# Products of zeros inside a stage of narrow products and around the first transposes, and the first half panel as two quarters

## The reference, cut to what matters

```python
k_cmp = compress_blocks(rope(kv[:, :, 0]), pe_k, w1_k, w2_k)    # 15 compressed keys of width 64 per group
s_c = jnp.einsum('bgrqd,bgcd->bgrqc', qb, k_cmp)                # compressed scores
p_c = masked_softmax(s_c, cmp_end[None, :] <= t[:, None])
o_c = jnp.einsum('bgrqc,bgcd->bgrqd', p_c.astype(v_cmp.dtype), v_cmp)
```

## Time and profile before

| | |
|---|---|
| runs | 2331.86 us median of 3 (2328.55 to 2335.62) |
| profiled execution | 2334.23 us, span from first to last instruction 2332.6 us |
| TensorE busy | 2076.8 us (89%), mean granted clock 0.971 |
| VectorE busy | 1424.1 us (61%) |
| ScalarE busy | 871.6 us (37%) |
| GpSimd busy | 1017.5 us (44%) |
| moved by DMA | 752.66 MB, 323 GB/s over the span |

### The profile page before, as it was taken

How to read it: one execution, slowest core, us unless ns; L and a number is a source line. 1 busy time by engine, 2 the same in 40 slices (tenths; PEclk the granted TensorE clock), 3 DMA queues, 4 the chain that set the end, 5 groups by cost and what they waited for, 6 DMA issues and landing times.

```text
span 2332.6 us, 24219 instructions
## 1 busy us (share of the span) xinstructions
PE 2076.8 (89%) x7378; PEld 1198.3 (51%) x7378; DVE 1424.1 (61%) x2980; ACT 871.6 (37%) x2116; POOL 1017.5 (44%) x1104
## 2 busy tenths in 40 slices
PE   7989999999999987898978998886999998878776
PEld 6768877778868643453423443342445444222222
DVE  3674464554477579774576654476846558684445
ACT  3544444645434332652223252223325223222222
POOL 0200000100000047677467566556755756777774
PEclk9999999999999899999999999998999999999999
DMA  8435545155545679999999999999999999999997
GB/s 315 171 124 174 190 161 205 50 190 180 180 145 185 271 319 409 344 396 412 414 410 409 416 411 412 411 414 396 401 415 387 413 413 409 410 409 409 409 410 310
DMA packets 172558, 752.66 MB, mean 323 GB/s; under 512 B 19184, under 2 KB 19472, under 8 KB 152864
## 3 DMA queue, kind: packets, MB, share of 16 engines
q0 software_dynamic: 148640, 544.05, 58.9%
q1 hardware_dynamic: 22224, 198.37, 22.7%
q10 hardware_dynamic: 1584, 8.91, 1.0%
HBM read 750.18 MB, written 4.22 MB: 323 GB/s over the span
## 4 chain that ended last, share of the span: by engine, by line
PE 49%; DMA 19%; DVE 12%; POOL 9%; issue 8%; ACT 2%; DVEq 1%; POOLq 0%; ACTq 0%; SPq 0%
PE ps L998 13%; DMA Z<-v,experts 10%; PE ps L731 8%; PE ps L733 8%; PE ps L732 8%; DMA Z<-u,experts 7%; PE ps L1018 6%; DVE Z L2039 5%; POOL Z L2413 4%; POOL Z L2428 3%; POOL ring L2428 1%; DMA ring<-panels 1%; PE ps L1075 1%; DVE ring_lo L1850 1%; DMA ring<-v,experts 1%
## 5 line engine op out<-in xcount | busy, mean ns | idle before, releaser
L998 PE MATMUL ps<-Z 128*128 128x512 f32 x1792 | 853.7, 622 | 157.8 <-DMA Z<-v,experts 95.4
L2039 DVE CUSTOM_DVE_ANT_0 Z<-Z,ps 128x1024 f32<-128x1024 f32 x512 | 612.0, 1219 | 408.6 <-DMA Z<-u,experts 402.1
L998 PEld LDWEIGHTS ps<-Z 128*128 128x128 f32 x1792 | 335.8, 197 | 635.4 <-issue 393.6
L2413 POOL DMA_INDIRECT Z<-u,experts x512 | 489.7, 956 | 293.0 <-issue 138.1
L2428 POOL DMA_INDIRECT Z<-v,experts x448 | 430.8, 962 | 252.0 <-PE ps L998 145.9
L1850 DVE TENSOR_TENSOR ring_lo<-ring,ring_hi 128x1024 fp32r<-128x1024 f32 x212 | 247.9, 1221 | 195.8 <-ACT ring_hi L1311 195.5
L1470 ACT ACTIVATE hdot<-hdot 128x4 f32<-128x4 f32 x128 | 26.3, 205 | 655.5 <-DVE hdot L2039 655.3
L731 PE MATMUL ps<-ring_hi,xT_lo 128*128 128x512 f32 x592 | 237.9, 402 | 14.2 <-DVE xT_lo L1909 8.9
L1018 PE MATMUL ps<-ring,o 128*128 128x512 f32 x528 | 232.3, 593 | 1.4 <-ACT o L1498 1.4
L732 PE MATMUL ps<-ring_lo,xT 128*128 128x512 f32 x592 | 232.9, 393 | 0.0
L733 PE MATMUL ps<-ring_hi,xT 128*128 128x512 f32 x592 | 232.7, 393 | 0.0
(11 more groups left out here) (285 smaller groups left out, 2152.0 us busy)
## 6 DMA issues: line engine op xcount, KB each, us to landing
ring<-panels SPq DMA_DIRECT2D x106, 1024.0 KB, 5.0
ring<-panels SPq DMA_DIRECT2D x37, 2048.0 KB, 10.4
Z<-u,experts POOLq DMA_INDIRECT x512, 12.1
Z<-v,experts POOLq DMA_INDIRECT x448, 12.8
Z<-panels SPq DMA_DIRECT2D x3, 2048.0 KB, 21.8
gain<-gains ACTq DMA_DIRECT2D x4, 1024.0 KB, 4.7
bias_lines<-bias_line POOLq DMA_DIRECT2D x1, 3072.0 KB, 13.8
gain<-gains ACTq DMA_DIRECT2D x5, 512.0 KB, 6.8
```

Of the source, the lines that this page charges most:

```text
L998: last = mm(ps[:, c, :], diag[s], vrow[s][:, c * NC:(c + 1) * NC], start=slot == 0, stop=slot == SLOTS - 1 or n == SUMMED[-1] - 1)
L2039: v.tensor_tensor_reduce(out=row, in0=row, in1=dotted, scale=1.0, scalar=0.0, op0=ALU.mult, op1=ALU.add, accum_out=hdot[:, t, slot:slot + 1])\
L2413: g.indirect_dma_start(out=urow[s], out_offset=None, in_=(u0, u1)[layer], in_offset=bass.IndirectOffsetOnAxis(ap=experts[:, t, slot:slot + ...
```

## The change

Two semaphores are new. SyncE asks for the first half panel as two transfers of 512 KB, chunk 0 and chunk 1, each with its own semaphore, and ScalarE waits for each before its cast. ScalarE copies the first token tile before all chunks (`early` is 0), and VectorE makes the low parts of the tokens before all chunks. TensorE runs four products of 128 columns of zeros before the first transposes (after a wait for the clearing of `zero`) and eight behind them, by a new helper, `waiting`, into bank 7. In the compressed scores it runs one product of 512 columns of zeros (`idle(1, 0)`, into bank 0) ahead of pairs 0 and 4 of each token tile, four in all.

```diff
@@ -487,6 +487,8 @@
         phase_end = sem("phase_end")
         tokens_landed = [sem(f"tokens{t}_landed") for t in range(TILES)]
         ident_landed = sem("ident_landed")
+        first_quarter_landed = sem("first_quarter_landed")
+        zero_set = sem("zero_set")
         consts_landed = sem("consts_landed")
         lam_dots = sem("lam_dots")
         loaded = sem("loaded")
@@ -650,7 +652,8 @@
 
             sp.dma_start(ident, consts[:, 0:P]).then_inc(ident_landed, 16)
             load_tokens(0)
-            load(0, 0, 0)
+            sp.dma_start(ring[:, 0, 0:CH], panels[0, :, 0:CH]).then_inc(first_quarter_landed, 16)
+            sp.dma_start(ring[:, 0, CH:2 * CH], panels[0, :, CH:2 * CH]).then_inc(landed[0][0], 16)
             load_tokens(1)
             load(0, 1, 0)
             for dst, src in ((cst[:, P:], consts[:, P:]), (xn[:, 0, 0:2 * LINE], line_consts), (rb[:, :], rel_bias),
@@ -719,6 +722,10 @@
 
                 for _ in range(n):
                     mm(ps[:, to, :], zero[:, :], const("upto"), start=True, stop=True)
+
+            def waiting(n):
+                for _ in range(n):
+                    mm(ps[:, 7, 0:P], zero[:, :], zero[:, :], start=True, stop=True)
 
             def second_tile():
                 if NORMED[turns]:
@@ -1169,6 +1176,8 @@
                             to = bank(key)
                             for t in range(TILES):
                                 for pair in range(PAIRS):
+                                    if pair % 4 == 0:
+                                        idle(1, 0)
                                     at = (t * PAIRS + pair) * 2 * CW
                                     last = mm(to[:, at:at + 2 * CW], turned_q[t][:, pair, :], kcT[:, pair // 2, :, :],
                                               start=True, stop=True)
@@ -1266,8 +1275,13 @@
                     if not SKEWED[turns]:
                         if NORMED[turns]:
                             idle(3)
+                        if turns == 0:
+                            pe.wait_ge(zero_set, 1)
+                            waiting(4)
                         transposed(turns, 0)
-                        if turns > 0:
+                        if turns == 0:
+                            waiting(8)
+                        else:
                             idle(2)
                 elif step == "dense":
                     if WIDTH[arg] == 2:
@@ -1306,7 +1320,9 @@
 
                 slot = (first + rel) % 2
                 for c in steps:
-                    if c % 2 == 0:
+                    if rel == 0 and first == FIRST["in0"] and c < 2:
+                        act.wait_ge(landed[0][0] if c else first_quarter_landed, 16)
+                    elif c % 2 == 0:
                         act.wait_ge(landed[slot][c // 2], i4 * 8 + 16 * ((first + rel) // 2 + 1))
                     copy(ring_hi[:, slot, c * CH:(c + 1) * CH],
                          ring[:, slot, c * CH:(c + 1) * CH]).then_inc(hi_ready, 1)
@@ -1323,7 +1339,7 @@
 
             def evict_turned(call):
                 first, norm = FIRST[NEXT[call]], NORMED[call]
-                early = {None: 1, "heads": 3}.get(norm if norm is None else norm if norm == "heads" else 0, 2)
+                early = 0 if call == 0 else {None: 1, "heads": 3}.get(norm if norm is None else norm if norm == "heads" else 0, 2)
 
                 def copies(t):
                     for b in range(2):
@@ -1919,6 +1935,9 @@
                     variance(1)
                     lower(name, 0, steps=[3])
                     normalize(1, norms, norm[1])
+                elif call == 0:
+                    lows(0)
+                    lower(name, 0)
                 else:
                     lower(name, 0, steps=[0])
                     lows(0)
@@ -2306,7 +2325,7 @@
             norms, turns, done, mlps, roots = 0, 0, 0, 0, 0
             for (step, arg), meets in zip(SCHEDULE, MEETS):
                 if step == "setup":
-                    v.memset(zero[:, :], 0.0)
+                    v.memset(zero[:, :], 0.0).then_inc(zero_set, 1)
                     v.memset(logf8[:, :, :], 0.0)
                     for s in PRIMED:
                         v.memset(stat[:, 0:1], 0.0).then_inc(s, AHEAD)
```

## The result

The changed kernel takes 2335.06 us (median of 22, 2331.40 to 2346.36), the kernel before 2331.44 us (median of 22, 2328.48 to 2337.14). The ratio is 1.0025, with a 95% interval of 1.0015 to 1.0034: a slowdown of 3.6 us by the medians, where 4.3 us less was forecast. The 22 times are not one heap. Fourteen lie between 2331.4 and 2338.3, and eight between 2341.8 and 2346.4. I call the times above 2340 us the upper group. The kernel before has none in its 22, nor in any of its 155 executions on record (highest 2339.49). The profiled execution took 2333.71 us with a span of 2331.9, so it shows the lower group.

The account below looks back on a forecast made before the run. It took the DMA to bound the last two thirds and TensorE to set the pace near 770 us. Start -1.6 and middle -2.7 gave -4.3 us, from 2331.86 to 2327.6 us; range 2322.5 to 2334.

Parts of the forecast that it names:

- -1.6 for the start: First token tile: would end at 16.3 us instead of 17.90, bounds nothing to -2.0 us.
- -2.7 for the middle: Compressed scores through H1: gelu would start 2.7 to 2.8 us earlier; -2.7 taken, bounds +3.7 and -2.8.
- hidden under VectorE: Eight zero products behind the first transposes: 1.8 us at the high clock, costing nothing while VectorE works.
- the queue is full until then and the bytes are the same: Start: splitting the first half panel would not delay the second, whose cast starts at 11.26 us.
- the place of the clock in c0: Compressed scores: clock falls at about 768.65 us, after 1.5 us of narrow products, read from one execution.
- The first product: Start: first product at about 9.7 us instead of 10.63, -0.9 us, with 0.23 us spacing.
- The zeros ahead of the transposes: Start: four zero products take 1.8 us, from 3.1 to 4.9, hidden under the tokens' arrival at 5.05.
- So both move.: After the first tile: the panel landing at 48 us and the bias broadcast move with the start's 1.6 us gain.
- rival (2): Start's gain swallowed by the panel landing at 48 us; only -2.7 us, so 2329.2; chance 0.09.
- The price of c0: Compressed scores: four zero products add 3.44 us; 6.96 us at the high clock against 5.57, ending 1.39 us later.
- What it gives back: Behind the compressed scores: clock stays high, O4 through H1 run faster; gelu starts 2.7 to 2.8 us earlier net.
- Rival (1): Compressed scores: zeros don't hold the clock, which falls inside them; net +3.7 us, 2334.0 with the start; chance 0.14.

Follow-up runs that it names:

- start_only: Changed kernel without the zeros in the scores, keeping the start's quarters, order and twelve zero products: 2333.83 us, ratio 1.0014 to the kernel before.
- middle_only: Kernel before with only the four zero products in the compressed scores added: 2330.94 us against 2331.11, ratio 0.9998.
- no_start_zeros: Changed kernel without the twelve zero products around the first transposes; quarters, new order and scores' zeros stay: 2331.06 us, ratio 0.9998.
- eight_zeros_again: Kernel before with new order, scores' zeros and the eight zero products behind the first transposes, half panel whole, a repeat: 2330.81 us, ratio 1.0000.
- four_zeros: Kernel before with new order, scores' zeros and only the four zero products ahead of the first transposes, half panel whole: 2330.20 us, ratio 0.9994.
- after_third: The changed kernel, unaltered, measured once more: 2333.53 us, three of 12 above 2340; its profile is of the lower group.
- whole_half: Changed kernel with the first half panel as one 1 MB transfer again; all zeros and new order stay: 2334.29 us, ratio 1.0017.
- order_and_middle: Kernel before with only the new order on ScalarE and VectorE and the scores' zeros; half panel whole: 2330.16 us, ratio 0.9992.

## Why the prediction was wrong, point by point

**The steps that failed.** The forecast was a sum of two gains, -1.6 us for the start and -2.7 for the middle, each priced alone and on one trace. Each was then measured alone, beside the same 35 runs of before. The start, start_only, is +2.7 us (2333.83 against 2331.11) where -1.6 was forecast. The middle, middle_only, is -0.2 us (2330.94), with an interval of -3.0 to +2.3 that holds both nothing and the forecast. The first step that failed is the price of nothing for the eight zero products behind the first transposes ("hidden under VectorE"). Without the start's zeros the same kernel has a ratio of 0.9998 and no time above 2333.8 (no_start_zeros); with them 15 of 51 executions lie some 10 us above the rest. The second is "the queue is full until then and the bytes are the same". The third is the place of the clock in c0, taken from one execution.

**The first product.** Right in the profile: 9.89 for 9.7, with 0.23 us from product to product. In the eight profiles of the changed kernel it comes at 9.89 to 10.37. That the clock rose near 7, as taken, is in part luck: the sixteen records of the eight zeros take 1.95 to 3.05 us in these profiles, and in eight_zeros_again they take 3.62 and the first product is still slow (0.76 us).

**The zeros ahead of the transposes.** Right: hidden, 3.06 to 4.93 for the forecast 3.1 to 4.9, and four_zeros, which has only these four at the start, is not slower than before.

**"The queue is full until then and the bytes are the same."** Wrong. With the split the cast of chunk 2 starts between 12.22 and 13.11 us in the ten profiles of kernels that have it, mean 12.5; without, at 11.25 to 12.17 in ten, mean 11.5. The transfer of quarters costs about 1 us of the second half panel. The prediction weighed a page of the Trainium skill (DMA: Bandwidth & Descriptors, Anatomy of one DMA) that states about 2 us fixed in each DMA and took the traces' back-to-back transfers as the answer to it. The page gives the figure for DMAs that GpSimd issues; these are asked for by SyncE. The sign of that rule was right, its size is halved by the measurement, and what is seen is a lower rate at nearly the same DMA share (323 GB/s for 398, means of ten), not a pause. In two of the profiles, start_only and after_third, TensorE lost the clock behind the wait as well. The length of the wait does not decide it: after_third waited 1.93 us and lost the clock, the first profile 2.18 us and kept it. The term -1.6 became -0.4 to +1.4 in the eight profiles of the changed kernel by the start of the second transposes (17.49 to 19.28 us, mean 17.92, against 17.90 before), so on average nothing. With the half panel whole and zeros at the start they come at 16.5 to 17.4. What the split costs in the end is less sure. The medians of the times below 2340 are 2333.6 (changed kernel, 36 of its 51 runs) against 2332.4 (whole_half), and 2331.06 (no_start_zeros) against 2330.16 (order_and_middle), about 1 us each, inside the scatter. The first gather comes at 833.2 us on average in the ten profiles with the split, at 831.5 in the ten without, ranges overlapping.

**"So both move."** Mostly right for the panel: its cast moved with the second transposes within 1.1 us in the profiles. In the changed kernel it starts at 47.7 to 49.9 us (mean 48.7, for 48.14 before and the forecast 46.5), because there was no gain to hand on. With the half whole and zeros at the start it is at 46.9 to 48.0, so rival (2) is not what happened. Beyond it nothing can be followed: the shift at c0's start varies from -5.0 to +3.4 us against the one profile of before, since the clock falls at other places on the way (near 50, 120, 655 and 690 us) from one execution to the next. A gain of 1 us at the start is lost in this.

**The price of c0.** Right: 7.07 for 6.96. **What it gives back**: -2.5 us in 12 profiles, -1.0 in 5, against the profile of before; -2.7 was forecast. The mechanism is the one described where the clock is high when c0 begins, as it is in all 17 profiles with zeros in the scores. Against a whole set of runs of before, though, it is worth little: middle_only gives 0.9998. The one trace of before, 20.91, lies between the 19.28 and the 24.07 that plain scores also take, so the gain was sized by one execution.

**Rival (1).** Its condition was too narrow. The prediction gave the zeros' failure 0.14 and a net of +3.7, by letting the clock fall inside c0. No profile with zeros in the scores shows that: where the clock falls, c0 is done. What was not considered is that the clock can be low before c0 begins. Then the stretch takes 24.07 us with plain scores, and the four zero products, 0.86 each at the high clock, take 1.72 each: some 6.9 us more, less about 1 us that H1 no longer runs slow, makes 30 by this estimate. That is 11 to 12 us above 18.39. The upper group of the kernels with zeros lies 10 to 12 us above the rest of their times, and that of the two kernels with plain scores 5 to 6 us, as 24.07 lies 5.7 above 18.39 and 4.8 above 19.28. The distances fit. The amount of low clock fits in kind: the profile of plain scores is low for 20.4 us here, which with the zeros would be about 27, by the same estimate. The 17 profiles with zeros average 1 us, so an execution of the upper group would have some 26 us more, where the recorded clocks give about 21. But it is argued, not shown. No profile of the upper group with zeros in the scores was caught in 17, and the execution with the 24.07 us took 2334.07 in all, short of its kernel's own group at 2336.4 and 2337.0.

**How often.** Kernels with both the eight (or fourteen) zero products at the start and the four in the scores have 27 of 111 executions above 2340 us. Kernels with the scores' zeros and without the eight have 1 of 45. Kernels with eight at the start and plain scores have 0 of 24 there, and 6 between 2336 and 2339.1. The kernel before, with neither, has 7 of 155 above 2336. So the eight raise the share of late executions, from 1 in 22 or fewer to 1 in 4, and the scores' zeros raise what one of them costs, from 5 or 6 us to 10 or more. The prediction, costing each edit by itself, could not see that. Why the eight products at 7 us decide about the clock at 762 us is open. The instants at which the clock turns lie elsewhere against the program in each of the 20 profiles, as the Trainium skill (TensorE: Matmul & The Clock Gate, Part 1) says that they vary between runs. In the five profiles without the eight, the first products are slow until the clock first rises, which may tie the program's later times to these instants. With the eight (or fourteen) the clock is high before the first product in 14 of 15, and the tie would be gone. That is a guess that no run tests.

**The sum.** Lower group: about +2 us against before, of which the split may have 1 or 2, and the rest is not resolved. Upper group: +12 us against before in 15 of 51 executions, 10 above the lower group, which alone lifts the mean by 3 us. The range and the sign of the forecast assumed one distribution, shifted.

## A version that is not slower

order_and_middle takes 2330.16 us, ratio 0.9992 (0.9983 to 1.0000) to before, and its 11 times lie within 3.7 us, where before's 35 of that set spread over 9.4. four_zeros is the same by its interval. They beat the changed kernel; against before the gain is at the edge of what was measured.

## What to carry to other kernels

A product of zeros that holds the clock would cost twice as much, by the estimate above, where the clock is already low: look at how a stretch of narrow products is entered, in more than one profile, before it is padded. A stretch whose length depends on the clock has several lengths in the same kernel; one profile shows one of them, so compare single times, not only their median, before and after. A transfer split for an early start can take its time from the transfer behind it.

## What was not expected of the hardware

Two transfers of 512 KB in packets of 4096 bytes, in place of one of 1 MB in packets of 8192, lowered the rate between 5.0 and 7.5 us from 398 to 323 GB/s (means of ten profiles each) with the DMA share nearly the same, 0.96 for 0.98. Zero products that fill a wait near the start and cost nothing there came with a share of executions 10 us slower of about 1 in 4, against 1 in 45 without them.
